# Half-block weight loads, unequal row rings, a rearranged prologue, VectorE two dots behind, and diagonals for latent tile 0, in a two-layer diffusion backbone with product-key experts

## The reference

```python
def layer(x, mod, P, rope, k_ext, v_ext):          # D_MODEL = 1024
    sh_m, sc_m, g_m, sh_f, sc_f, g_f = jnp.split(mod, 6, axis=-1)
    h = rmsnorm(x, P['norm_mix_g']) * (1.0 + sc_m) + sh_m
    proj = h @ P['w_in']                           # 1024 x 2048
    attn = attention(q, k, v)                      # latents: rotary, 128 cached keys
    hy = hyena(proj[..., V_END:HY_END], P)         # gated long convolution by FFT
    sg = chunk_gmlp(proj[..., HY_END:], ...)
    x = x + g_m * (jnp.concatenate([attn, hy, sg], axis=-1) @ P['w_out'])
    h = rmsnorm(x, P['norm_ffn_g']) * (1.0 + sc_f) + sh_f
    return x + g_f * peer(h, ...)

def peer(h, wq, keys, u_tab, v_tab):               # per token: 8 heads x top 16 experts
    s = einsum(q, keys)                            # 2 x 128 scores per head
    ...                                            # top 16 of each, top 16 of the 256 sums
    a = gelu(einsum('td,ted->te', xt, u_tab[idx])) # one row of 1024 per expert
    return einsum('te,ted->td', gate * a, v_tab[idx])
```

## Time and profile before

| | us |
|---|---|
| median of 3 runs | 4637.51 |
| lowest and highest run | 4630.89, 4637.74 |
| the profiled execution | 4663.97 |
| its span, first to last instruction | 4662.2 |
| TensorE (PE) busy | 3442.7 |
| VectorE (DVE) busy | 2632.0 |
| ScalarE (ACT) busy | 1122.8 |
| POOL busy (issuing indirect DMAs) | 2806.0 |
| DMA engines, mean rate | 323 GB/s, 1503.70 MB |

### The profile page before, as it was taken

One profiled execution on the slowest core, in us unless ns is written; L12 is line 12 of the kernel. 1 busy time (PEld: TensorE's weight loads), 2 busy tenths in 40 slices (PEclk: granted clock), 3 DMA queues, 4 the chain that ended last, 5 costly groups with the idle time before them and its releaser, 6 DMA issues.

```text
span 4662.2 us, 37811 instructions
## 1 busy us (share of the span) xinstructions
PE 3442.7 (74%) x11256; PEld 1602.1 (34%) x11256; DVE 2632.0 (56%) x6503; ACT 1122.8 (24%) x2533; POOL 2806.0 (60%) x2564
## 2 busy tenths in 40 slices
PE   7869868766577767777776898786766676677777
PEld 3733434323123334332222444442322222222223
DVE  2166656456455565556666565564665666666661
ACT  3423223121212222212121432231211212121212
POOL 0035555566555666667777344565667777777774
PEclk8889888888788888889889899888878999998899
DMA  7468898789999999899999687887899999999997
GB/s 295 143 234 301 311 338 296 278 301 336 346 367 341 358 341 336 332 359 363 348 352 360 216 286 297 318 307 282 327 334 352 356 365 354 357 362 347 367 358 279
DMA packets 394680, 1503.70 MB, mean 323 GB/s; under 512 B 44396, under 2 KB 46126, under 8 KB 376432
## 3 DMA queue, kind: packets, MB, share of 16 engines
q0 software_dynamic: 368640, 1342.34, 78.9%
q1 hardware_dynamic: 25840, 158.96, 8.8%
HBM read 1498.24 MB, written 2.88 MB: 322 GB/s over the span
## 4 chain that ended last, share of the span: by engine, by line
POOL 30%; PE 24%; issue 18%; DMA 17%; DVE 7%; ACT 3%; SPq 0%; another core or an unknown queue 0%; DVEq 0%; POOLq 0%; ACTq 0%
POOL rows_ring L605 16%; POOL rows_ring L616 14%; DMA rows_ring<-in_peer_v,idx 7%; DMA rows_ring<-in_peer_v,turned_idx 7%; PE psum L928 6%; PE psum L920 5%; DVE rows_ring L1465 3%; PE psum L854 3%; PE psum L706 3%; DMA rows_ring<-in_peer_u,idx 2%; DMA ring<-in_ada 1%; PE psum L651 1%; PE psum L693 1%; PE psum L839 1%; PE psum L886 1%
## 5 line engine op out<-in xcount | busy, mean ns | idle before, releaser
L605 POOL DMA_INDIRECT rows_ring<-in_peer_u,idx x1280 | 1453.1, 1135 | 1198.5 <-DVE rows_ring L1465 587.3
L928 PE MATMUL psum<-rows_ring,diag 128*128 128x512 f32 x3072 | 1591.3, 667 | 634.0 <-DMA rows_ring<-in_peer_v,idx 581.4
L1465 DVE SCALAR_TENSOR_TENSOR rows_ring<-rows_ring,area 128x1024 f32<-128x1024 f32 x1280 | 1549.5, 1223 | 718.9 <-DMA rows_ring<-in_peer_u,idx 679.7
L928 PEld LDWEIGHTS psum<-rows_ring,diag 128*128 128x128 f32 x3072 | 618.4, 212 | 1567.2 <-issue 1453.3
L616 POOL DMA_INDIRECT rows_ring<-in_peer_v,idx x768 | 812.1, 1057 | 297.8 <-issue 211.3
L920 PE MATMUL psum<-rows_ring,diag 128*64 128x512 f32 x2048 | 641.1, 757 | 385.4 <-DMA rows_ring<-in_peer_v,turned_idx 376.8
L616 POOL DMA_INDIRECT rows_ring<-in_peer_v,turned_idx x512 | 540.5, 1056 | 334.2 <-PE psum L920 180.3
L1165 ACT ACTIVATE diag<-ident,turn 128x128 f32<-128x128 f32 x768 | 303.3, 401 | 1663.0 <-PE psum L928 1189.1
L920 PEld LDWEIGHTS psum<-rows_ring,diag 128*64 128x64 f32 x2048 | 160.4, 161 | 712.5 <-issue 661.5
L706 PE MATMUL psum<-area,ring 128*128 128x128 f32 (+1 forms) x832 | 240.9, 446 | 6.5 <-DMA ring<-in_win 6.5
L1474 DVE SCALAR_TENSOR_TENSOR turn<-acts,gate_s,gate_e 128x16 f32<-128x16 f32 x80 | 18.8, 235 | 382.3 <-ACT acts L1135 233.6
(11 more groups left out here) (185 smaller groups left out, 2864.3 us busy)
## 6 DMA issues: line engine op xcount, KB each, us to landing
ring<-in_ada SPq DMA_DIRECT2D x48, 1024.0 KB
ring<-in_win SPq DMA_DIRECT2D x32, 1024.0 KB
ring<-in_wout SPq DMA_DIRECT2D x24, 1024.0 KB
ring<-in_wq SPq DMA_DIRECT2D x24, 1024.0 KB
rows_ring<-in_peer_u,idx POOLq DMA_INDIRECT x1280
ring<-in_dft SPq DMA_DIRECT2D x12, 1024.0 KB
rows_ring<-in_peer_v,idx POOLq DMA_INDIRECT x768
rows_ring<-in_peer_v,turned_idx POOLq DMA_INDIRECT x512
```

Source lines behind the costliest of these rows:

```text
L605: pool.indirect_dma_start(row(0, k), None, peer_u, bass.IndirectOffsetOnAxis(ap=idx[v % IDX_PLACES][:, k:k + 1], axis=0)).then_inc(row_lan ...
L928: m = pe.matmul(acc[:, b, :], diag[:, (r + j) % 4, :], row(1, r + j)[:, b * 512:(b + 1) * 512], start=first and j == 0, stop=last and j == 1)
L1465: dve.scalar_tensor_tensor(out=row(0, k), in0=row(0, k), scalar=1.0, in1=h, op0=ALU.mult, op1=ALU.mult, accum_out=dots[:, k:k + 1]).then_i ...
```

## The change

Nothing that is computed changes, apart from how sums of tile 0 are brought together.

- **Half blocks.** `ring` has five places of 128 x 1024 (0.5 MB) in place of four of 128 x 2048. Each projection has a block of its own, modulation n has four, the DFT steps have four each. `STREAM` follows from the order of first use, and a place is free after its block's last use.
- **Row rings.** `ROWS = (5, 6)`: five places for U, six for V, fetched as far ahead; `spread` stays four rows ahead. `rows_ring` grows from 8 to 11 rows, `ring` shrinks by as much.
- **Prologue.** Only modulation 0 to 3 stands ahead of the context mixer, 4 to 9 lie between its jobs, 10 and 11 come behind the first unit's pick. The latent stream's rms and filter move into the latent stretch. The half blocks of modulation 0 to 9 of layer 0 are loaded into the eleven places of `rows_ring`, which no row uses yet. Eight of them go ahead of the constants; the latents' part of `xT`, `swap` and `cos_sin` are loaded later, ahead of the first `wq` block.
- **VectorE behind.** VectorE has its own list `DVE_ORDER`: in every stretch all its jobs but `dot` and `pick` come two dots later than in `ORDER`. The sums of the dots have two buffers, so that `dot(v, 0)` waits for gelu of unit v - 2 only. The last part, behind the last stretch, keeps its order.
- **Tile 0.** `paired` holds for the context's units alone; latent tile 0 uses 128 x 128 diagonals.

```diff
-SLOTS = 4
-ROWS = 4
+HALF = BLOCK // 2
+SLOTS = 5
+ROWS = (5, 6)
...
     if st == C_ and l == 0:
-        jobs = js("mod:0 mod:1 modT:0 mod:2 modT:1 mod:3 modT:2 mod:4 modT:3 rms:0 mod:5 modT:4 f1:0 mod:6 modT:5 f2:0 ")
-        jobs += latent("rms:0") + js("mod:7 modT:6 f3:4 mod:8 modT:7 hf:4") + latent("f1:0") + js("mod:9 modT:8")
-        jobs += latent("f2:0") + js("mod:10 modT:9 mod:11") + latent("f3:0 f3:1 f3:2 f3:3") + js("modT:10 modT:11")
...
+        jobs = js("mod:0 mod:1 modT:0 mod:2 modT:1 mod:3 modT:2 f1:0 modT:3 rms:0 f2:0 mod:4 f3:4 qk:0 modT:4 vt:4 hf:4 hs:0 "
+                  "hy:0 mod:5 ko:0 hy:1 modT:5 hy:2 hy:3 mod:6 hy:4 hy:5 modT:6 su:0 ut:0 su:1 mod:7 qk:1 sp:0 hs:1 modT:7 "
+                  "qk:2 hs:2 qk:3 mod:8 sp:1 hs:3 qk:4 modT:8 df:4 hs:4 mod:9 cv:0 cv:1 modT:9")
...
 def paired(grp, u):
-    return u < PEER_HEADS
+    return GROUPS[grp][1] == C_
...
-        unit("down", v + (k + ROWS) // TOPK, (k + ROWS) % TOPK)
+        unit("down", v + (k + ROWS[0]) // TOPK, (k + ROWS[0]) % TOPK)
...
-            pair("up", r + ROWS)
-            pair("spread", r + ROWS)
+            pair("up", r + ROWS[1])
+            pair("spread", r + 4)
...
+_late = [("mod", 0, C_, 10), ("mod", 0, C_, 11), ("modT", 0, C_, 10), ("modT", 0, C_, 11)]
+ORDER, _taken = input_jobs(0, C_) + output_jobs(0, C_, 0) + _first + _late, 0
+DVE_ORDER = list(ORDER)
+def behind(jobs, n):
+    out, held, dots = [], [], 0
+    for job in jobs:
+        if job[0] in ("dot", "pick", "down", "up"):
+            while held and held[0][0] <= dots:
+                out.append(held.pop(0)[1])
+            dots += job[0] == "dot"
+            out.append(job)
+        else:
+            held.append((dots + n, job))
+    return out + [job for _, job in held]
+def stretch(mixer, upto, also=0):
...
+    jobs = weave(mixer, _steps[_taken:end])
+    ORDER += jobs
+    DVE_ORDER += behind(jobs, 2)
...
+for _block, _ in STREAM:
+    if _block[:2] == ("ada", 0) and _block[3] < 40:
+        _p, _n_rows = SLOTS + _n_rows % sum(ROWS), _n_rows + 1
+    else:
+        _p, _n_ring = _n_ring % SLOTS, _n_ring + 1
...
-                if n == SLOTS:
+                if n == 8:
                     small_loads(0)
                     const_loads()
...
+                if (kind, l, st, i) == ("wq", 0, C_, 0):
+                    latent_loads()
...
             def dot(grp, u, k):
-                if v and k == 0:
-                    dve.wait_ge(s["gelu_ready"], v)
+                if v > 1 and k == 0:
+                    dve.wait_ge(s["gelu_ready"], v - 1)
...
-            for job in ORDER:
+            for job in DVE_ORDER:
```

More of the change, by code:

```diff
@@ L210, in weave @@
 def weave(mixer, experts):
-    total, cost, taken, out = sum(ROOM[j[0]] for j in mixer), 0, 0, []
+    total, cost, taken, out = sum(ROOM[j[0]] for j in mixer) or 1, 0, 0, []
     for job in mixer:
@@ L219, in weave @@
     return out + experts[taken:]
-_first = [("pick", 0, 0, p) for p in range(PICK_PARTS)] + [("gexp", 0, 0, 0)] + [("down", 0, 0, k) for k in range(ROWS)]
+_first = [("pick", 0, 0, p) for p in range(PICK_PARTS)] + [("gexp", 0, 0, 0)] + [("down", 0, 0, k) for k in range(ROWS[0])]
 _steps = [_job for _v in range(len(UNIT) + 2) for _job in step_jobs(_v)]
[L224 to L231, removed]
+_late = [("mod", 0, C_, 10), ("mod", 0, C_, 11), ("modT", 0, C_, 10), ("modT", 0, C_, 11)]
[13 more added lines that the diff above has]
+def stretch(mixer, upto, also=0):
+    global ORDER, DVE_ORDER, _taken
+    end = _steps.index(upto) + also
+    jobs = weave(mixer, _steps[_taken:end])
+    ORDER += jobs
+    DVE_ORDER += behind(jobs, 2)
     _taken = end
@@ L280 @@
 TURNED_BEFORE = {j: TURNED[i - 1] for i, j in enumerate(TURNED) if i}
[L283 to L305, removed]
-            for _i in range(2):
-                _b("dftu", _i, "df_mm", "df", 3)
-            for _i in range(2, 4):
-                _b("dftu", _i, "cv_mm", "cv", 1)
-        for _part, (_t, _end) in enumerate(PARTS[_st]):
-            for _i in range(4 * _part, 4 * _part + 4):
-                _b("wout", _i, "wo_mm", "wo", 2 * _i + 1)
-            for _i in range(4 * _part, 4 * _part + 4):
-                _b("wq", _i, "wq_mm", "wq", 2 * _i + 1)
-            _b("keys", _part, "kb_mm", "kb", 2 * _end - 1)
@@ L316, with blocks_of @@
-AT = {block: n for n, (block, _) in enumerate(STREAM)}
+def blocks_of(job):
+    kind, l, st, n = job
+    some = {"mod": ("ada", range(4 * n, 4 * n + 4)), "qk": ("win", [11 + n if n else 0]), "vt": ("win", range(1, 4)),
+            "hy": ("win", [4 + n]), "su": ("win", [10 + n]), "wo": ("wout", [n]), "wq": ("wq", [n])}
+    if st == L_:
+        some.update({"hf": ("dft", range(4)), "df": ("dftu", range(4)), "cv": ("dftu", range(4, 8))})
+    if kind in ("ka", "kb"):
+        some[kind] = ("keys", [1 if n > 1 else 0])
+    name, places = some.get(kind, ("", []))
+    return [(name, l, st, i) for i in places]
@@ new lines @@
+LAST_USE = {}
+for _job in ORDER:
+    for _block in blocks_of(_job):
+        LAST_USE[_block] = (_job[0] + "_mm", done(*_job))
+STREAM = list(LAST_USE.items())
+PLACES = SLOTS + sum(ROWS)
+PLACE, PLACED, FREED = [], {}, []
+_n_ring = _n_rows = 0
+for _block, _ in STREAM:
[3 more added lines that the diff above has]
+        _p, _n_ring = _n_ring % SLOTS, _n_ring + 1
+    _same = [n for n, (p, _) in enumerate(PLACE) if p == _p]
+    FREED.append(STREAM[_same[-1]][1] if _same else None)
+    PLACE.append((_p, len(_same)))
+    PLACED[_block] = PLACE[-1]
@@ L449, in mixer_peer_kernel @@
         gate_s = sb("gate_s", 4)
-        dots = sb("dots", TOPK)
+        dots = grid(sb("dots", 2 * TOPK)[:, :], 2)
         acts = sb("acts", TOPK)
```

156 lines of the change are left out of this document (83 added, 73 removed).

## The result

The changed kernel takes **4303.83 us** (median of 4 runs, 4296.51 to 4310.48). The kernel before takes 4637.62 in the same comparison. The ratio is 0.9271, with a 95% interval of 0.9231 to 0.9311. The gain is 334 us; the forecast had 107, and its range ended at 4425. The profiled execution took 4310.48 us; its span is 4308.7, against 4662.2 before.

What follows compares the result with a forecast made beforehand. It held that DMA at 357 GB/s bounds pure experts and engine coupling the woven stretches. Terms -54 + 20 - 25 - 10 - 30 - 8 + 10 - 10 + 0 = -107 took 4637.51 to 4530.5 us; range 4425 to 4640.

Steps and rivals of the forecast that it cites:

- The floor: Pure expert units 56 to 79: DMA engines 97% busy at 357 GB/s, taken as the floor, 46.6 us a unit.
- Rings and delay: VectorE two dots behind, longer rings: -25 (units 0 to 7), -10 (16 to 31), -30 (40 to 47), -8 (pure).
- the same coupling: Stretches with the mixer woven in: 325 us over the DMA traffic's time, lost to engines waiting for one another.
- Rival B: Woven stretches: rings decouple more, POOL's waits for VectorE mostly go, near the DMA floor, some 4400 us; chance 0.13.
- Prologue: Ahead of unit 0: fewer modulations and one rms before the first context projection, cv ends 54 us earlier, bounds 35 and 65.
- What returned: Units 0 to 7: latent rms, filter steps, modulation 10 and 11 and their loads move in, +20, between 0 and 38.
- Tile 0 by diagonals: Units 8 to 15 and 48 to 55: 105 us more TensorE work per layer, mostly absorbed; net -10 and 0.
- Rival C: Latent tile 0: TensorE becomes the bound and its extra work is exposed, slower, 4740 us; chance 0.10.
- Half blocks: Weight ring: five half-block places, 2.6 MB ahead for 4.2; PE has slack in layer 1, so no cost.
- Rival D: Layer 1 modulations, cv and filter: weights come late, up to 130 us on PE, 4595 to 4660 us; chance 0.10.
- The wait added on ScalarE: Woven units: the next unit's softmax step waits for w_ready, given two dots later; +10, upper bound 276.
- The signs it named: POOL's first wait, units 8 to 15, halved VectorE waits; wrong if weight-ring waits grew over 100 us or 8 to 15 passed 550.

Runs made afterwards that it cites:

- r8: Changed kernel with the prologue's old order and early latent loads, all else as changed: 4312.2 us, ratio 0.9251 to the kernel before.
- r15: Changed kernel without delay, tile 0 in pairs, latent rms and f1 to f3 spread among the context mixer's first jobs, latent loads earlier: 4262.3 us.
- r17: Changed kernel with tile 0 in pairs, latent rms and f1 to f3 among the context mixer's jobs behind hs:0, latent loads earlier, delay kept: 4273.2 us.
- r7: Changed kernel with latent tile 0 in pairs again, all else as changed: 4290.5 us, ratio 0.9204 to the kernel before.
- r5: Kernel before with half blocks in eight places, row rings 4 and 4 (also second dot buffer, modulation loads into row rings, latent filter steps side by side): 4636.4 us.
- r12: As r5 but with five half-block places in place of eight, row rings still 4 and 4: 4672.8 us, ratio 1.0041 to the kernel before.
- r4: Changed kernel with VectorE in the common order again (no two-dot delay), row rings 5 and 6: 4300.1 us, ratio 0.9264 to the kernel before.
- r10: As r12 (old prologue, pairs, no delay) but row rings 6 and 6 and four half-block places: 4334.6 us, ratio 0.9325 to the kernel before.
- r9: As r12 but row rings 5 and 6, and only 2 KB of each 4 KB row fetched and dotted; output not the reference's: 3996.6 us (one run).

## Why the prediction was wrong, point by point

**The floor (wrong; the step that failed).** The prediction took the DMA engines' 97% at 357 GB/s in units 56 to 79 for the floor, 46.6 us a unit, and built on it: 325 us in all were to be had, 27 of them in units 16 to 31, and next to nothing in experts alone. The runs show 382 GB/s there, 395 in units 16 to 31, and a unit of 44.0 us (POOL's issuing). Of the 246 us by which the profiled executions lie further apart than forecast, 186 are in the three stretches where, because of this floor, the forecast took 18 of the 204 us that came. The busy share of the DMA engines is no measure of how near a ceiling is: per share it was 357 / 0.97 = 368 GB/s before and 395 / 1.01 = 391 after, so the same busy time can carry 6% more bytes. What that part of the busy time was is not shown. The Trainium skill (DMA: Bandwidth & Descriptors, section Bandwidth) has 425 GB/s for one 16 MB load and 435 as the ceiling of the ports; the 395 of this trace lies under both, and beside either figure 357 was no floor. The same section also gives some 358 as the memory's limit for one core and says that it binds loads from there; the 395 GB/s that this trace holds for 769 us lie above it, so here the measurement decides. The profile of before had the hint as well: POOL busy 680.4 us of 900 with 188.7 of gaps, 97% full.

**Rings and delay (mechanism half right, size wrong by three).** The sum gave -25, -10, -30 and -8, and -25 and -20 of the same coupling inside the terms of tile 0: together -118, for both. The rings alone measured -347 to -384, the delay 0 beside them and -149 without. That VectorE's late steps hold POOL was right (without the delay and with long rings POOL still waits 460 us for it), but of the places where VectorE stands the prediction named the mixer's steps (sg_v), and not `weigh`, which comes 80 times and had 382 us of idle time in front of it in the profile of before. Nor did it see that the V ring matters most: it counted the two V rows and the U row as one thing. Rival B named the result, "the stretches come near the DMA floor", with 0.13, and took two thirds of the 325, 4400; all of them would have given 4278. So the measured 4304 lies within what its mechanism allows, but by luck in part: 66 us came from units 56 to 79, where it had nothing to give.

**Prologue (right in front, wrong behind).** POOL's first wait fell from 250.2 to 188.5, 62 us; forecast 54. What returned was put at +20 and measured 516 - 440 = +76 against r8, whose first wait is 258.8. The term counted the moved work's busy time, and took it that a stretch with idle time absorbs it. It left out that rms, `f1`, `f2` and `f3` wait for one another, and that nothing else of the mixer can go ahead of them. r15 to r17 fit this, and do not prove it beyond their intervals. Net: 4312.2 - 4303.8 = 8 us where the forecast had 34, and within the error: by the ratios r8 is even 0.2% ahead.

**Tile 0 by diagonals (right).** Of 105 us more in each layer, 5 and 14 us show (433 against 428 in r7, 406 against 392), forecast 15 and 20. TensorE was busy 387 of 433 us, at a granted clock of 0.94; forecast some 450 in no more than 480. With pairs in the same place (r7) it was busy 330 of 428, at 0.87:

```profile
698.00:1126.00 428.00, 330.32 (x1387) 154.06 (x1386) 266.12 (x643) 107.44 (x268) 287.15 (x259) 0.87 0.94 354
```

So the diagonals cost 57 us of busy time and not 105, at a higher granted clock. By the ratio of the two clocks, 387 us at 0.94 would be some 418 at 0.87 (an estimate), so the clock accounts for some 31 of the 48 us and the rest is not explained. Rival C did not come about. That most of the 105 us would be absorbed was right. The whole stretches gained 50 and 37 us and not 10 and 0, by the rings.

**Half blocks (the halving right, the places at nothing wrong by 1%).** r5 is 0.5% faster with eight places, r12 0.4% slower with five. So the halving costs nothing, and the three places that go cost some 1%, which the prediction put at nothing. The profiled executions of r5 and r12 lie 2.5 us apart and do not show where. Rival D as such did not show: TensorE's waits for weight blocks are 45 us before, and 60 after with those that land in the row ring. The Trainium skill's rule of 1 MiB or more per DMA (DMA: Bandwidth & Descriptors, section Bandwidth) is not borne out here, where blocks of 0.5 MB in eight places cost no time; a half block took 6.8 to 9.5 us (medians) from issue to landing in the changed kernel. The 2.0 us that the prediction takes from the Trainium skill's section Anatomy of one DMA stand there for DMAs that GpSimd issues, and these are issued by SP; its estimate of 280 us for 140 more loads was far off in any case.

**The wait added on ScalarE (too high).** Forecast +10. The softmax step did wait in the changed kernel, 158.4 us in all (38.9 in r4), and no cost shows, since r4, without the delay, takes the same time.

```profile
L1154 ACT ACT_TABLE_LOAD x79 | 101.4, 1283 | 158.4 <-DVE turn L1500 158.4
```

**The signs it named.** POOL's first wait fell to 188.5 (it said some 196). Units 8 to 15 show TensorE busy 387 us, not some 450, in 433. POOL's waits for VectorE fell from 587.3 to 151.9 us over the whole run, while its V fetches' waits for TensorE rose from 263.3 to 428.5. Neither sign of being wrong came, so the signs did not catch what was wrong: the size.

**Left open.** How far a fetch's 1.07 us on POOL depends on the transfers (below); what bounds units 16 to 31 once the rings are long; whether r10 loses by its rings or its places; where the three places of r12 cost; and whether the second buffer for the dots is needed for the gain.

## What to carry to other kernels

When engines run in order and hand work round in a ring, one or two more places in the buffer whose consumer is late can be worth more than any reordering. Try each ring by itself and both together, since their gains do not add up (here 20, 289 and 384 us). Small instructions where engines meet (here a 0.23 us product with 4.8 us of idle time ahead of it each time) are worth a look beside the groups with the longest busy time, but a wait at such a place can move without the time moving. Before a DMA share near 1 is called a floor, add the busy time and the issue gaps of the queue that starts the transfers; if they fill the window, that queue may be the bound, and a run with half the bytes tells. Work that is moved out of a prologue can return with its chain of dependences and not with its busy time alone, so look for jobs that do not need it and can stand between its links.

## What the runs showed of the hardware

A row fetch on POOL (128 rows of 4 KB, indices from SBUF) costs its queue 0.94 us at the least, with half the bytes too, and 0.30 us pass before the next. The fetches of U rows in experts alone, in the changed kernel and in r9 (least, median and longest ns, then the stretch):

```profile
L630 POOL DMA_INDIRECT rows_ring<-in_peer_u,idx x328: 933/938/1990, 3300.0 to 4198.5; - x164
```

```profile
L635 POOL DMA_INDIRECT rows_ring<-in_peer_u,idx x335: 942/949/1460, 2999.8 to 3898.2; - x168
```

Half the bytes leave the least and the median as they are; only the longest ones fall, from 1990 to 1460 ns. From issue to landing, the median of a U fetch over the whole run falls from 6.5 to 3.7 us:

```profile
rows_ring<-in_peer_u,idx POOLq DMA_INDIRECT x1280, 6.5
```

```profile
rows_ring<-in_peer_u,idx POOLq DMA_INDIRECT x1280, 3.7
```

And the same transfers, through the same queue, run at 357 GB/s with rings of four rows and at 382 with five and six.
